# A hybrid decoder step on one core: input and first weight slab ahead of all else, the first projection with its contraction outermost, and the bias products between the index blocks

## The reference, cut to what matters

```python
proj = x @ w_in                       # 1056 x 1024 @ 1024 x IN_COLS
qi = proj[..., o:o + 4 * 64]          # indexer queries, 4 heads x 64
ki = proj[..., o:o + 64]              # indexer key
wi = proj[..., o:o + 4] * 4 ** -0.5   # weight of each indexer head
...
scores = jnp.einsum('bthd,bsd->bths', qi, ki_all) * IDX_DIM ** -0.5
index = jnp.einsum('bth,bths->bts', wi, jax.nn.relu(scores))
index = jnp.where(visible[None], index, -jnp.inf)
_, sel = lax.top_k(index, topk)       # 256 keys of the prompt, 129 of a sample
k_sel, v_sel = gather(k_all, sel), gather(v_all, sel)
bias = rel_bias[t5_bucket(dist)]      # 32 buckets x 8 heads
logits = q . k_sel * HEAD_DIM ** -0.5 + bias
out = softmax(logits) . v_sel
...
# then RWKV-7 for the other 8 heads, output projection, layer norm,
# gated MLP with a causal convolution, layer norm
```

## Time and profile before

| what | value |
|---|---|
| median of 3 runs | 1823.06 us (1818.77 to 1823.41) |
| the profiled execution: its time | 1824.13 us |
| its span in the trace | 1822.4 us |
| TensorE busy | 1649.9 us, 91% of the span |
| VectorE, ScalarE, GpSimd busy | 922.4, 686.4, 337.3 us |
| mean granted TensorE clock | 0.944 |

### The profile page before, as it was taken

One profiled execution on the slowest core, in us unless ns is written; L12 is line 12 of the kernel. 1 busy time (PEld: TensorE's weight loads), 2 busy tenths in 40 slices (PEclk: granted clock), 3 DMA queues, 4 the chain that ended last, 5 costly groups with the idle time before them and its releaser, 6 DMA issues.

```text
span 1822.4 us, 40306 instructions
## 1 busy us (share of the span) xinstructions
PE 1649.9 (91%) x17398; PEld 1202.9 (66%) x17398; DVE 922.4 (51%) x2131; ACT 686.4 (38%) x1164; POOL 337.3 (19%) x209
## 2 busy tenths in 40 slices
PE   5959999998996378979878989999999999999997
PEld 2628666665775256766656866666666666888887
DVE  2089999995855556777631663223222333000027
ACT  4452332114665455666554133333333333312100
POOL 1330112102320111221202011111222111111100
PEclk9879999998999578898989989999999999999999
DMA  6210213234332211100203221111111110511001
GB/s 246 87 58 24 95 47 98 76 99 164 106 94 72 86 35 28 39 21 21 85 3 131 93 96 47 47 47 47 47 47 50 67 47 29 188 47 47 24 24 73
DMA packets 49794, 126.62 MB, mean 69 GB/s; under 512 B 17202, under 2 KB 23762, under 8 KB 41778
## 3 DMA queue, kind: packets, MB, share of 16 engines
q1 hardware_dynamic: 48530, 123.00, 19.9%
q0 software_dynamic: 1088, 1.05, 0.2%
HBM read 100.26 MB, written 23.77 MB: 68 GB/s over the span
## 4 chain that ended last, share of the span: by engine, by line
PE 83%; DVE 8%; ACT 5%; issue 2%; DMA 1%; SPq 1%; POOL 0%; DVEq 0%; ACTq 0%; POOLq 0%
PE bank L2110 79%; PE bank L2210 2%; DVE arena L2390 1%; PE bank L896 1%; PE bank L949 1%; DVE arena L1893 1%; SPq L840 1%; DVE arena L2375 1%; DVE arena L1923 1%; POOL arena L2548 0%; DVE arena L1889 0%; DVE arena L1896 0%; ACT L1322 0%; DMA arena<-slabs 0%; DVE arena L1890 0%
## 5 line engine op out<-in xcount | busy, mean ns | idle before, releaser
L2110 PE MATMUL bank<-arena 64*64 64x64 f32 (+10 forms) x16700 | 1565.1, 285 | 138.1 <-ACT arena L1288 26.7
L2110 PEld LDWEIGHTS bank<-arena 128*128 128x128 f16 (+6 forms) x16700 | 1124.4, 122 | 576.4 <-issue 141.9
L2548 POOL TENSOR_TENSOR arena<-arena 128x2048 f16<-128x2048 f32 x53 | 215.8, 4074 | 920.6 <-ACT arena L2264 885.1
L2436 DVE TENSOR_SCALAR_CACHE_REDUCE arena<-arena 128x384 bf16<-128x384 f32 (+6 forms) x231 | 196.9, 917 | 1.2
L2263 ACT ACTIVATE arena<-arena 128x2048 f16<-128x2048 f32 x53 | 100.7, 1899 | 166.7 <-PE bank L2110 143.5
L1966 DVE SCALAR_TENSOR_TENSOR arena<-bank,arena 128x512 f32<-128x512 f32 (+1 forms) x20 | 12.7, 636 | 213.0 <-PE bank L2110 213.0
L1934 DVE TENSOR_SCALAR arena<-arena 128x1072 f32<-128x1072 f32 x22 | 18.9, 857 | 187.8 <-issue 173.8
L2280 ACT ACTIVATE arena<-bank 128x352 f32<-128x352 f32 x75 | 34.6, 462 | 196.6 <-PE bank L2110 196.6
L2264 ACT ACTIVATE arena<-arena 128x2048 f32<-128x2048 f32 x53 | 100.4, 1895 | 0.0
L1684 POOL TENSOR_TENSOR arena<-arena 128x512 f32<-128x512 f32 x40 | 55.7, 1401 | 223.2 <-ACT arena L1277 111.7
L1946 DVE SCALAR_TENSOR_TENSOR arena<-bank,arena 128x352 f32<-128x352 f32 (+1 forms) x66 | 33.9, 514 | 120.4 <-PE bank L2110 93.6
(11 more groups left out here) (258 smaller groups left out, 1167.2 us busy)
## 6 DMA issues: line engine op xcount, KB each, us to landing
arena<-slabs SPq DMA_DIRECT2D x53, 1024.0 KB, 5.0
arena<-kcache SPq DMA_DIRECT2D x32, 256.0 KB, 2.9
arena<-vcache SPq DMA_DIRECT2D x32, 256.0 KB, 3.0
prw<-arena SPq DMA_DIRECT2D x42, 176.0 KB, 1.9
arena<-xt SPq DMA_DIRECT2D x4, 1056.0 KB, 10.5
x1d<-arena SPq DMA_DIRECT2D x8, 512.0 KB, 2.6
arena<-x1d SPq DMA_DIRECT2D x1, 4096.0 KB, 13.0
y<-arena SPq DMA_DIRECT2D x8, 512.0 KB, 2.6
```

The source lines that it names most:

```text
L2110: return nc.tensor.matmul(out, lhsT, rhs, start=start, stop=stop, skip_group_check=True)
L2436: last = dve.tensor_scalar(junk, a, s, None, op, ALU.add, accum_out=cnt[:, k:k + 1])
L2548: pool.tensor_tensor(WL[r].rearrange("p a b -> p (a b)"), STG[s], WH[r].rearrange("p a b -> p (a b)"), ALU.subtract).then_inc(slab_lo, 1)
```

## The change

Only the first stage is reordered; apart from the place of one table and the points at which the engines wait, nothing later changes.

- SyncE issues slab 0 first, then the four quarters of the input, then slab 1, and only then the constants and tables. The bias round trip through HBM comes before slab 6 instead of before slab 2.
- ScalarE splits slab 0 ahead of the input's quarters, and slab 1 behind them. Slab 2 goes between the evictions of slabs 0 and 1, slab 3 in front of the index blocks, slabs 4 and 5 behind `sindex`.
- VectorE makes the low part of the input ahead of the small tables. GpSimd splits slab 0 without waiting for `x_lo` or the page table; those waits stand behind split 3, ahead of the `kidx` transfers.
- `first_cols` computes slab 0 with six banks open: for each quarter of the input, all six banks' share.
- The eight bias products follow index blocks 2 to 9, the samples' bias blocks 10 and 11, on TensorE and on ScalarE (`BIAS_STEPS`). `BST` moves to where the first half of the raw input lay.

```diff
+INDEX_BLOCKS = [(j, k0) for j in range(TQ) for k0 in range(0, P * (j + 1), 512)]
+BIAS_STEPS = {**{2 + h: ("bias", h) for h in range(H)}, 10: ("sbias", 0), 11: ("sbias", 1)}
...
+    for n, (j, k0) in enumerate(INDEX_BLOCKS):
+        for h in range(IH):
+            b.add(("index", j, k0, h), "act")
+        if n in BIAS_STEPS:
+            b.add(BIAS_STEPS[n], "act")
...
-        BST = words(G0 + KT * TOK + 3 * P + NT * LS + NT * H * NT + H * P, H, 3 * P)
+        BST = words(G0, H, 3 * P)
...
-            for w in range(4):
-                if w == 2:
+            load_slab(0)
+            for q in range(4):
+                sp.dma_start(XF[:, 2 * q:2 * q + 2, :], i["xt"][:, 2 * q:2 * q + 2, :]).then_inc(x_in[q], 16)
+            load_slab(1)
+            sp.dma_start(CON, i["consts"]).then_inc(consts_in, 16)
+            sp.dma_start(PAR, i["params"]).then_inc(consts_in, 16)
+            sp.dma_start(RB[0:NBUCKET], i["rb"]).then_inc(consts_in, 16)
+            sp.dma_start(PTB, i["page_table"]).then_inc(pt_in, 16)
+            sp.dma_start(OHT[0:NBUCKET], i["oht"]).then_inc(tables_in, 16)
+            sp.dma_start(OHS[0:NBUCKET], i["ohs"]).then_inc(tables_in, 16)
+            load_slab(2)
+            load_slab(3)
+            emptied(sp, ("col", SL_KI, 0, 2))
+            sp.dma_start(o["kit"], KI[0:D, :]).then_inc(kit_out, 16)
+            for w in range(4, SL_RW + 5):
+                if w == 6:
                     emptied(sp, ("bias", H - 1))
                     sp.dma_start(biasd, BST.rearrange("p a b -> p (a b)")).then_inc(bias_out, 16)
                     sp.wait_ge(bias_out, 16)
                     skew = bass.AP(biasd.tensor, biasd.offset + P - 1, [[3 * P * H - 1, P], [3 * P, H], [1, 2 * P]])
                     sp.dma_start(BIAS, skew).then_inc(bias_in, 16)
-                load_slab(w)
-            emptied(sp, ("col", SL_KI, 0, 2))
-            sp.dma_start(o["kit"], KI[0:D, :]).then_inc(kit_out, 16)
...
-            pe.wait_ge(tables_in, 32)
-            pe.wait_ge(tables_ready, 2)
-            for h in range(H):
+            def bias(h):
                 b = open_bank(pe, ("bias", h))
                 mm(b[:, 0:3 * P], RBW[0:NBUCKET, h, :], OHT[0:NBUCKET, :], True, True).then_inc(filled, 1)
-            for k, (k0, kn) in enumerate(((0, PAST), (PAST, NS))):
+            def sbias(k):
+                k0, kn = ((0, PAST), (PAST, NS))[k]
                 b = open_bank(pe, ("sbias", k))
                 for q in range(NT):
                     last = mm(b[0:H * NT, 0:kn], RBI[0:NBUCKET, q, :], OHS[0:NBUCKET, q, k0:k0 + kn], q == 0, q == NT - 1)
...
-            pe.wait_ge(x_lo, 4)
-            cols(SL_QI)
+            def first_cols(w):
+                pe.wait_ge(slab_lo, w + 1)
+                r = w % NRING
+                bs = [(m, n, open_bank(pe, ("col", w, m, n))) for m in range(2) for n in range(3)]
+                for q in range(4):
+                    pe.wait_ge(x_lo, q + 1)
+                    for m, n, b in bs:
+                        c, s = slice(P * m, P * m + P), slice(CH3 * n, CH3 * n + CH3)
+                        for k in (2 * q, 2 * q + 1):
+                            mm(b[:, 0:CH3], WH[r][:, k, c], XH[:, k, s], k == 0, False)
+                            mm(b[:, 0:CH3], WH[r][:, k, c], XL[:, k, s], False, False)
+                            last = mm(b[:, 0:CH3], WL[r][:, k, c], XH[:, k, s], False, k == KT - 1)
+                        if q == 3:
+                            last.then_inc(filled, 1)
+            first_cols(SL_QI)
...
             emptied(pe, ("col", SL_KI, 0, 2))
-            for (j, k0, kn) in IJ:
+            for n, (j, k0, kn) in enumerate(IJ):
                 for h in range(IH):
                     b = open_bank(pe, ("index", j, k0, h))
                     s = slice(D * (h % 2), D * (h % 2) + D)
                     mm(b[:, 0:kn], QI[s, h // 2, P * j:P * j + P], KI[s, k0:k0 + kn], True, True).then_inc(filled, 1)
+                if n == 2:
+                    pe.wait_ge(tables_in, 32)
+                    pe.wait_ge(tables_ready, 2)
+                if n in BIAS_STEPS:
+                    {"bias": bias, "sbias": sbias}[BIAS_STEPS[n][0]](BIAS_STEPS[n][1])
...
-            act.wait_ge(tables_ready, 3)
-            for h in range(H):
+            def bias(h):
                 b = wait_job(act, ("bias", h))
                 act.activation(BST[:, h, :], b[:, 0:3 * P], ACT.Copy).then_inc(freed["act"], 1)
-            for k, (k0, kn) in enumerate(((0, PAST), (PAST, NS))):
+            def sbias(k):
+                k0, kn = ((0, PAST), (PAST, NS))[k]
                 b = wait_job(act, ("sbias", k))
                 act.activation(SBIAS[0:H * NT, k0:k0 + kn], b[0:H * NT, 0:kn], ACT.Copy).then_inc(freed["act"], 1)
-            for q in range(4):
-                act.wait_ge(x_in[q], 16)
-                act.activation(XH[:, 2 * q:2 * q + 2, :], XF[:, 2 * q:2 * q + 2, :], ACT.Copy, scale=XS).then_inc(x_hi, 1)
...
-            for w in range(3):
-                split(w)
+            split(0)
+            for q in range(4):
+                act.wait_ge(x_in[q], 16)
+                act.activation(XH[:, 2 * q:2 * q + 2, :], XF[:, 2 * q:2 * q + 2, :], ACT.Copy, scale=XS).then_inc(x_hi, 1)
+            split(1)
             cols(SL_QI, lambda m: QI[:, m, :])
-            split(3)
+            split(2)
             cols(SL_KI, lambda m: KI, (0,))
             rows(SL_KI, lambda t, tn: WI[0:tn, t, :], IH, UN * IH ** -0.5)
-            split(4)
+            split(3)
+            act.wait_ge(x_lo, 4)
             n = 0
-            for (j, k0, kn) in IJ:
+            for nb, (j, k0, kn) in enumerate(IJ):
                 for h in range(IH):
                     b = wait_job(act, ("index", j, k0, h))
                     if n >= 3:
                         act.wait_ge(index_read, n - 2)
                     act.activation(RL[:, n % 3, 0:kn], b[:, 0:kn], ACT.Relu, scale=D ** -0.5).then_inc(freed["act"], 1)
                     n += 1
-            split(5)
+                if nb in BIAS_STEPS:
+                    {"bias": bias, "sbias": sbias}[BIAS_STEPS[nb][0]](BIAS_STEPS[nb][1])
             for k, (k0, kn) in enumerate(((0, PAST), (PAST, NS))):
                 b = wait_job(act, ("sindex", k))
                 act.activation(SRL[:, k0:k0 + kn], b[:, 0:kn], ACT.Relu, scale=D ** -0.5).then_inc(freed["act"], 1)
-            act.wait_ge(bias_in, 16)
+            split(4)
+            split(5)
             for w in (SL_V, SL_V + 1):
                 rows(w, lambda t, tn: VT[0:tn, t, SLAB * (w - SL_V):SLAB * (w - SL_V) + SLAB], SLAB)
                 split(w + 4)
             emptied(act, ("row", SL_V + 1, TQ))
             act.wait_ge(filled, plan.number(("sisum", 1)) + 1)
+            act.wait_ge(bias_in, 16)
...
+            for q in range(4):
+                dve.wait_ge(x_hi, q + 1)
+                dve.scalar_tensor_tensor(XL[:, 2 * q:2 * q + 2, :], XF[:, 2 * q:2 * q + 2, :], XS,
+                                         XH[:, 2 * q:2 * q + 2, :], ALU.mult, ALU.subtract).then_inc(x_lo, 1)
...
             dve.sem_inc(tables_ready, 3)
-            for q in range(4):
-                dve.wait_ge(x_hi, q + 1)
-                dve.scalar_tensor_tensor(XL[:, 2 * q:2 * q + 2, :], XF[:, 2 * q:2 * q + 2, :], XS,
-                                         XH[:, 2 * q:2 * q + 2, :], ALU.mult, ALU.subtract).then_inc(x_lo, 1)
-            dve.wait_ge(bias_in, 16)
...
-            pool.wait_ge(pt_in, 16)
             pages = lambda b, g: pool.value_load(PTB[0:1, PG * b + g:PG * b + g + 1], min_val=0, max_val=NPOOL - 1)
-            pool.wait_ge(x_lo, 4)
...
             for w in range(4):
                 split(w)
+            pool.wait_ge(pt_in, 16)
+            pool.wait_ge(x_lo, 4)
```

20 lines of the change are left out of this document (2 added, 18 removed).

## The result

| | before | after |
|---|---|---|
| median, same chip, 4 runs each | 1820.91 us (1817.45 to 1823.41) | 1797.57 us (1796.05 to 1797.96) |
| the profiled execution: time, span | 1824.13, 1822.4 us | 1796.05, 1794.4 us |
| mean granted TensorE clock | 0.944 | 0.945 |

The changed kernel is faster: ratio 0.9869, 95% interval 0.9849 to 0.9889. Forecast were 1797.0 us and a range of 1790 to 1804. The terms that led there are less exact than their sum, and two of them err against each other; so I read the same views again, in the same order. The kernel before has a fourth run here, of 1817.45 us, which lowers its median by 2.15 us: the medians lie 23.3 us apart, the two profiled executions 28.1.

What follows compares the result with a forecast made beforehand. The start-up before the values' projection at 131.22 us was taken as the bound, its end passed on one to one. Index keys limit the gain to 26.1 us: 1824.13 - 26.1 = 1798.0 profiled, 1797.0 median; range 1790 to 1804.

Steps and rivals of the forecast that it cites:

- Slab 0 lands at 7.1: Start: the first transfer, issued at 0.9 us, lands between 5.8 and 8.4; the middle, 7.1, was taken.
- TensorE starts at 17.2, held by split 0: First projection: first low part held by GpSimd's split 0 to 14.9; TensorE starts at 17.2 instead of 40.33, 23.1 us earlier.
- Rival (a): Index keys are no bound, 1792.6 us; or the first low part is not held, 1794.9; chance 0.15.
- No further pause, the work to the last small bank unchanged: First projection: TensorE never waits after the first quarter; last small bank evicted at 57.2 instead of 80.34.
- Split 3 holds VectorE's first step to 65.1: Index stage: VectorE's first accumulating step meets GpSimd's split 3 and is held to 65.1, 4 us.
- Bias products cost nothing, because VectorE covers them: Index blocks: ScalarE's 4.6 us and TensorE's 8.8 us of bias work covered by VectorE's steps; bounds nothing to 8.8, taken nothing.
- Rival (c): Index blocks: bias products exposed, 8.8 us of TensorE less 4.4 covered by the keys: 4.4, 1801.4 us; chance 0.07.
- The keys come last, at 101.8: Index stage: last key lands at 101.8, 4.4 us after VectorE is ready; `sindex` waits for it, 26.1 us earlier.
- Values' projection at 105.1: Behind the index stage: the values' projection starts 26.1 us earlier, at 105.1 instead of 131.22.
- Selection covers splits 4 and 5: Selection: the two splits cost 0 to 2.9 us; 0 taken, since the first counting pass runs beside most of them.
- Rival (d): The selection becomes the bound: 2.9 us for two splits, up to 3 more from splits 6 and 7: 1803; chance 0.06.
- Rival (e): TensorE stays at the slow spacing: 1826.9 us in the first projection only, chance 0.03; 1848 throughout, chance 0.04.

Runs made afterwards that it cites:

- 7: The kernel of experiment 6 with seven of the eight bias products left out and zeros written by a memset, so its bias is not the reference's: 1787.31 us.
- 8: The kernel of experiment 6 with both of the samples' bias products behind the last index block: 1788.29 us, ratio 0.982 to the kernel before.
- 4: The changed kernel, but GpSimd issues the 32 index keys and the samples' weights before split 3: 1793.11 us, ratio 0.9849 to the kernel before.
- 5: The changed kernel, but six bias products ahead of the first index block, the other two and the samples' two behind earlier blocks: 1796.48 us.
- experiment 6: The changed kernel, but ScalarE splits slab 3 directly behind slab 2, before evicting slab 1: 1788.74 us, ratio 0.9818 to the kernel before.

## Why the prediction was right

The frame was as forecast: a start-up whose end is passed on one to one, and a first projection that starts 24.4 us earlier (forecast 23.1). In the index stage, though, one step of the forecast was wrong, and it came out only because it stood beside a wait of nearly the same length. Nor is the agreement of the time itself (1797.57 for 1797.0) closer than luck: single runs of one kernel differ by 2 to 8 us, and the median from which I counted moved by 2.15 with one more run. Step by step:

- *Slab 0 lands at 7.1* (5.8 to 8.4): measured 5.74, the early bound. In all nine traces with the slab first it is 4.85 to 5.12 us after issue, like a slab alone, though a stream stands behind it. This term was 1.3 us off. The first half of the rule in the Trainium skill ("DMA: Bandwidth & Descriptors", queues, rings and completion order), that descriptors are consumed in ring order, would have given exactly this.
- *TensorE starts at 17.2, held by split 0*: 15.97, with the hold of 2.2 as priced. Rival (a), no hold, was wrong.
- *No further pause, the work to the last small bank unchanged*: right; evicted at 55.84 instead of 57.2, 1.4 earlier.
- *Split 3 holds VectorE's first step to 65.1*: 59.70 to 63.65; right in kind, 1.4 earlier.
- *Bias products cost nothing, because VectorE covers them*: wrong. VectorE stood idle 4.8 us. Rival (c) had this mechanism with a price of 8.8 less 4.4. The premise that failed is "VectorE's steps cover both": over the whole stage they do, but the cover is decided block by block, with a ring of three buffers between ScalarE and VectorE (my reading of the gaps; no run changed the ring). 1.5 us of the 4.8 fall at 70 to 74 us, where the clock comes up from 0.50 and the stock is small, 3.2 behind the samples' product. Experiments 7 and 8 show that the second kind hangs on that product's place.
- *The keys come last, at 101.8*: they landed at 100.4: issued 1.2 earlier with the whole stage, and landed 0.2 quicker. VectorE, forecast for 97.4, came 1.5 earlier with the stage and 4.8 later by its idle time: 97.4 - 1.5 + 4.8 = 100.7. So `sindex` is released by VectorE and not by the keys. My own test for this step ("I am wrong if `sindex` waits for VectorE") came out against me, by 0.3 us.
- *Values' projection at 105.1*: 104.08. What saved the forecast is that the unpriced 4.8 us filled the 4.4 us which the keys left free. Rival (c) had that cover in its price, but that it fitted so closely was luck: had the keys not been late, the same omission would have cost the forecast all of the 4.8 us. The 1.0 us that is left is the earlier landing (1.3) less the 0.3 by which VectorE came behind the keys. Experiments 4 and 5 show both sides of the tie.
- *Selection covers splits 4 and 5*: their cost at the attention is nothing, as taken, but not for my reason, see below; VectorE's spare time of 5.23 us lies just outside the 1 to 5 that I had given as a sign. Rival (d) did not occur.
- *Rival (e), half pace throughout*: the pace recovered within 4 us, as in the earlier trace rows; the index blocks ran at clock 1.00 from 74 to 90 us, after 0.50 from 58 to 70.

With 27.14 in place of 26.1 the sum is 1824.13 - 27.14 = 1796.99 for a measured 1796.05. The rest, 0.94, is within the scatter behind the start-up.

## What to carry to other kernels

Price a filler between steps of a pipeline per step against the stock that the consumer has there, not in total against its busy time. Where a wait is moved away, look which wait ends next to it: here two ended within 0.3 us, and the edit that moved both brought 8.0 us (experiment 6), the one that moved mainly the keys 1.1 (4). When an elementwise GpSimd instruction of 4 us can fall anywhere, put it where VectorE is idle, as split 3 does in experiment 6, not in front of its first step.

## What the runs showed that I had not expected

**The selection falls in step with GpSimd's splits.** VectorE's spare time before the attention was 5.21 to 5.25 us in all twelve traces, with values' starts from 95 to 131 us, with or without two more splits in the selection. In the kernel after, the steps that met a split (normally 0.17) and the last split:

```profile
113.06 2.19 DVE L2468 TENSOR_SCALAR arena<-arena 128x7 f32<-128x7 f32 x1
...
159.03 3.88 DVE L2481 TENSOR_TENSOR arena<-arena 128x7 int32<-128x7 f32 x1
...
311.89 1.57 DVE L2481 TENSOR_TENSOR arena<-arena 128x7 int32<-128x7 f32 x1
```

```profile
309.37 4.07 POOL L2570 TENSOR_TENSOR arena<-arena 128x2048 f16<-128x2048 f32 x1 [17.40 <-ACT arena L2282]
```

Splits come every 21.48 us, and three rounds of the selection take 20.07 (a step that isn't held recurs every 6.69). So from its third meeting with a split on the selection arrives a little early, is held to the split's end, and goes on from there; the second hold, 3.3 to 3.9 us in the versions, takes up whatever phase it had. The last held step ends with the last split, at 313.46 and 313.44, and from that end to the first step of the attention it is 78.23 to 78.25 us in all twelve traces. By the kernel's waits the splits follow TensorE's slabs, so VectorE's end is tied to TensorE's. A split more or less in front cost nothing here.

**What a split holds.** Not only steps with two sources: the multiplication by a scalar at 59.70, one source, took 3.95 us instead of 0.29. The Trainium skill ("GPSIMD Engine Reference", specifications) names contention with VectorE instructions in a 2-port mode or with two inputs from SBUF; the trace agrees for both kinds if this form counts as 2-port. The counting passes, which also have one source, ran beside splits 4 and 5 and kept their pace. In the rows these two kinds differ in their rate: the multiplication takes 0.29 us for 128 elements a partition and 0.49 for 512, the counting pass 0.56 for 384 and 1.22 for 1024, so 0.52 and 1.03 ns for each further element.

**A small transfer waits beside a large one.** The samples' weights' write (0.5 KB, GpSimd's queue, issued at 87.89) held up the next issue for 4.92 us in 6, where SyncE's read-back of the bias (1 MB, issued at 87.12, 6.1 us to landing) ran beside it; the 1.5 MB bias write, issued at 81.20, had just ended. In the kernel after, where the read-back is issued at 92.44 and the weights' write only at 99.03, it was 1.39. In 7, where the bias traffic starts at 62.84 instead of 81.20, it was 1.53. The last index key (32 KB, same queue) shows the same: 5.1 us to landing in 6 and 4.7 in 8, 1.9 to 2.1 in the kernel after and in 7. The Trainium skill ("DMA: Bandwidth & Descriptors", queues, rings and completion order) says that a semaphore's increment lands only after every earlier write of the same DMA engine, across its queues; these numbers agree, without showing single DMA engines.

**The clock at the samples' product.** During and behind the samples' product (32 x 512, weights 32 x 32) the granted clock fell in the kernel after:

```profile
88.00:90.00 2.00, 2.00 (x6) 0.53 (x5) 1.89 (x4) 1.30 (x3) 0.82 (x2) 1.00 1.16 476
90.00:92.00 2.00, 2.00 (x5) 0.61 (x5) 0.99 (x2) 0.59 (x1) 0.52 (x1) 0.79 0.84 329
92.00:94.00 2.00, 2.00 (x8) 0.67 (x4) 0.08 (x1) 0.78 (x2) 0.87 (x2) 0.50 0.37 61
```

TensorE was busy all the time by its own column. At 2.4 GHz before, it was at 1.2 GHz from 92 us on, and VectorE's longest idle time, 2.89 us, ends at 93.92. It fell there in eight of the nine traces that have this product between the blocks, in 7 for instance, whose product is evicted at 82.62, to 0.96 from 78 to 82 and 0.61 from 82 to 86. But in 6 it stayed at 1.00 until 88 us with the same product at the same place, so the product alone does not decide it, and the cause stays open. In 8, which has it behind the blocks, the clock stayed at 1.00 to 88 us as well.

**Scatter behind the change.** From the values' start to the last stage of TensorE the untouched middle took 938.5 to 947.3 us in the twelve traces. A difference of 2 or 3 us between spans is no evidence on the start-up.
